# A two-layer fp32 transformer trunk: four slots of split weights, written-out FFN groups, and a new sharing of weight splits between VectorE and GpSimd

## The reference, cut to what matters

```
layer 0:  x = LN(alpha*x + causal_attention(x @ w_qkv) @ w_o)      # 16 heads of 64, partial rotary
layer 1:  x = LN(alpha*x + diff_attention(x @ w_q, x @ w_kv) @ w_o) # 8 heads, two score maps each
both:     up, gate = split(x @ w_in)                                # 1024 -> 2 * 2816
          up = causal_conv3(up) + b;  x = LN(alpha*x + (gelu(up) * gate) @ w_out)
```

## Time and profile before

| what | us |
| --- | --- |
| median of 3 runs | 638.14 (637.22 to 638.71) |
| the profiled execution's own time | 634.84 |
| its span | 633.0 |
| TensorE busy | 613.4 (97% of the span) |
| VectorE busy | 447.4 (71%) |
| ScalarE busy | 335.8 (53%) |
| GpSimd busy | 63.9 (10%) |

### The profile page before, as it was taken

How to read it: one execution, slowest core, us unless ns; L and a number is a source line. 1 busy time by engine, 2 the same in 40 slices (tenths; PEclk the granted TensorE clock), 3 DMA queues, 4 the chain that set the end, 5 groups by cost and what they waited for, 6 DMA issues and landing times. The chain is left out here.

```text
span 633.0 us, 9437 instructions
## 1 busy us (share of the span) xinstructions
PE 613.4 (97%) x3317; PEld 507.1 (80%) x3317; DVE 447.4 (71%) x800; ACT 335.8 (53%) x550; POOL 63.9 (10%) x85
## 2 busy tenths in 40 slices
PE   8999999999999999999889999989999999999995
PEld 6777777798888888889768788768988888888894
DVE  5657477577777777777786676668776777777786
ACT  5667567446444444456326785863545544455450
POOL 4400000420000000000340020044000000000002
PEclk9999999999999999999999999999999999999998
DMA  8973334444555555555368434443634555555521
GB/s 291 338 249 134 134 133 135 134 134 133 200 199 199 199 199 183 174 177 183 146 203 302 160 134 133 134 134 121 211 110 168 188 183 174 176 196 199 199 67 68
DMA packets 68682, 109.67 MB, mean 173 GB/s; under 512 B 2044, under 2 KB 47404, under 8 KB 68140
## 3 DMA queue, kind: packets, MB, share of 16 engines
q1 hardware_dynamic: 68012, 105.09, 49.0%
q0 software_dynamic: 640, 4.20, 1.7%
HBM read 108.23 MB, written 1.05 MB: 173 GB/s over the span
## 5 line engine op out<-in xcount | busy, mean ns | idle before, releaser
L798 DVE TENSOR_TENSOR w_lo<-raw,w_hi 128x2048 fp32r<-128x2048 f32 (+1 forms) x115 | 206.0, 1804 | 68.8 <-ACT w_hi L594 68.8
L594 ACT ACTIVATE w_hi<-raw 128x2048 fp32r<-128x2048 f32 (+1 forms) x125 | 182.0, 1495 | 37.7 <-PE wide L1087 37.7
L1270 PE MATMUL score<-xT,w_hi 128*128 128x512 f32 x288 | 103.2, 401 | 1.5 <-DVE w_lo L798 1.1
L1085 PE MATMUL wide<-w_hi,xT 128*128 128x512 f32 (+1 forms) x256 | 98.4, 384 | 1.9 <-DVE w_lo L856 0.8
L1087 PE MATMUL wide<-w_hi,xT 128*128 128x512 f32 (+1 forms) x256 | 93.4, 365 | 0.0
L1086 PE MATMUL wide<-w_lo,xT 128*128 128x512 f32 (+1 forms) x256 | 93.0, 363 | 0.0
L1272 PE MATMUL score<-xT,w_lo 128*128 128x256 f32 x288 | 80.5, 280 | 0.0
L733 ACT ACTIVATE conv<-up_sum,conv_cols 128x256 f32<-128x256 f32 x36 | 21.7, 602 | 97.1 <-DVE up_sum L997 97.1
L1270 PEld LDWEIGHTS score<-xT,w_hi 128*128 128x128 f32 x288 | 54.0, 188 | 19.2 <-issue 7.2
L1085 PE MATMUL wide<-w_hi,hT_hi 128*128 128x512 f32 x176 | 68.8, 391 | 0.0
L1087 PE MATMUL wide<-w_hi,hT_lo 128*128 128x512 f32 x176 | 68.7, 390 | 0.0
(11 more groups left out here) (181 smaller groups left out, 992.1 us busy)
## 6 DMA issues: line engine op xcount, KB each, us to landing
raw<-in_ffn_w_in SPq DMA_DIRECT2D x44, 1024.0 KB, 5.1
raw<-in_ffn_w_out SPq DMA_DIRECT2D x22, 1024.0 KB, 4.9
raw<-in_a_w_qkv SPq DMA_DIRECT2D x9, 1024.0 KB, 7.0
raw<-in_w_kv_shared SPq DMA_DIRECT2D x8, 1024.0 KB, 5.1
raw<-in_a_w_o SPq DMA_DIRECT2D x4, 1024.0 KB, 4.8
raw<-in_b_w_q SPq DMA_DIRECT2D x4, 1024.0 KB, 5.0
raw<-in_b_w_o SPq DMA_DIRECT2D x4, 1024.0 KB, 4.9
raw<-in_a_w_qkv SPq DMA_DIRECT2D x6, 512.0 KB, 8.7
```

Of the source, the lines that this page charges most:

```text
L594: ins = nc.scalar.activation(w_hi[slot][:, part], raw[slot][:, part], ACT.Copy)
L798: ins = nc.vector.tensor_tensor(w_lo[slot][:, part], raw[slot][:, part], w_hi[slot][:, part].bitcast(F32), ALU.subtract)
L1085: nc.tensor.matmul(dst, a_hi, b_hi, start=start, stop=False, skip_group_check=True)
L1270: nc.tensor.matmul(parts, w_hi[slot][:, cols], xT[:, :, kt, :], start=kt == 0, stop=False, skip_group_check=True)
```

## The change

1. `w_hi` and `w_lo` get four slots (`RING = 4`). `raw` keeps three (`RAW_RING = 3`). The high split of c now waits for TensorE's use of c - 4, the load of c still for the low split of c - 3. In the scheduler of layer 0 the first chunk to be split by the list stays 3 (`FIRST`), which now has a slot without any wait for TensorE.
2. To make room, FFN tiles lie in attention tiles: `hT_hi` and `hT_lo` in `oT_hi` and `oT_lo`, and `conv`, `gelu`, `hidden`, `up_sum`, `gate_sum` in `headT` (named qT and kT in listings).
3. Groups 2 to 9 of the FFN are written out on every engine instead of looped.
4. Splits around the norms: chunk 17 (66) joins the mixer's list of high splits. At n = 1 GpSimd splits both halves of 49 and the second half of 50 before the variance of st = 0, and the first half of 51 before that of st = 1, and none behind `std_inv`. VectorE splits the first half of 50 (`split_shared_lo`), the second half of 51 and all of 52.
5. At the end of layer 0, TensorE's second products of row half 1 run chunk by chunk (chunk 47 first, then 48) instead of column half by column half, its transposes 2 and 3 move ahead of the four products of column group 1 that run early, and VectorE takes one statistics step after a low split of `xT`.

```diff
@@ constants @@
-RING = 3
+RAW_RING = 3
+RING = 4
@@ mixer_schedule @@
-    for c in range(first_chunk + RING, first_chunk + 17):
+    splits = range(first_chunk + (FIRST if A else RING), first_chunk + 18)
+    for c in splits:
         for half in range(2):
-            after[("split_hi", c, half)], after[("split_lo", c, half)] = [], [("split_hi", c, 1)]
+            after[("split_hi", c, half)] = []
+            if c < first_chunk + 16:
+                after[("split_lo", c, half)] = [("split_hi", c, 1)]
...
+        if c - RING in uses:
+            after[("split_hi", c, 0)].append(uses[c - RING])
@@ yoco_trunk @@
-                POOL_SPLITS[2 * layer + 1, st] = ([(c + 2 * st, 0)], [(c + 2 * st, 1)])
+                POOL_SPLITS[2 * layer + 1, st] = ([(c, 0), (c, 1), (c + 1, 1)] if st == 0 else [(c + 2, 0)], [])
...
+        hT_hi = [oT_hi[:, 2 * b:2 * b + 2, :] for b in range(2)]
+        hT_lo = [oT_lo[:, 2 * b:2 * b + 2, :] for b in range(2)]
+        conv = headT[0][:, 0:2, :]
+        gelu = headT[0][:, 2:4, :]
+        hidden = headT[0][:, 4:6, :]
...
@@ SyncE @@
-                elif not isinstance(c, int) or c >= RING:
-                    sp.wait_ge(lo_done, c - RING + 1)
+                elif c >= RAW_RING:
+                    sp.wait_ge(lo_done, c - RAW_RING + 1)
+                slot = c % RAW_RING
@@ ScalarE @@
+                act.wait_ge(raw_in[c % RAW_RING], 16 * (c // RAW_RING + 1))
+                if c >= RING:
                     act.wait_ge(chunk_used, c - RING + 1)
...
                 c = base + QKV_CHUNKS + WO_CHUNKS
-                split_static(c + 1)
                 xT_hi_part(2 * layer + 1, (0, 1))
-                split_static(c + 2)
+                split_hi(c + 2)
                 xT_hi_part(2 * layer + 1, (2, 3))
+                split_hi(c + 3)
...
                 ffn_group(1, "second")
-                with act.Fori(2, GROUPS - 1) as i:
-                    ffn_group(i, "loop")
+                for i in range(2, GROUPS - 1):
+                    ffn_group(i, "middle")
@@ VectorE @@
+            def split_shared_lo():
+
+                part = slice(0, CHUNK // 2)
+                dve.wait_ge(shared_hi_done, 1)
+                nc.vector.tensor_tensor(w_lo[SHARED % RING][:, part], raw[SHARED % RAW_RING][:, part],
+                                        w_hi[SHARED % RING][:, part].bitcast(F32), ALU.subtract).then_inc(shared_lo_done, 1)
...
+                    elif peeled == "last" and cg + RING == SHARED:
+                        split_shared_lo()
@@ TensorE @@
-                        if layer and (cg, kt, st) in ((0, 0, 0), (1, 2, 0)):
+                        if layer and (cg, kt, st) in ((0, 0, 0), (1, 0, 0)):
...
-                for i, st, half in ([(GROUPS - 2, 0, 0), (GROUPS - 2, 0, 1), (GROUPS - 1, 0, 0), (GROUPS - 1, 0, 1)]
-                                    + [(i, 1, half) for half in range(2) for i in (GROUPS - 2, GROUPS - 1)]):
+                tail = [(GROUPS - 2, 1, 0), (GROUPS - 2, 1, 1), (GROUPS - 1, 1, 0), (GROUPS - 1, 1, 1)]
+                if layer + 1 == LAYERS:
+                    tail = [tail[n] for n in (0, 2, 1, 3)]
```

More of the change, by code:

```diff
@@ L128, in mixer_schedule @@
         previous = step
-    for c in range(first_chunk + RING, first_chunk + 17):
-        after[("split_hi", c, 0)].append(uses[c - RING])
+    for c in splits:
+        if c - RING in uses:
+            after[("split_hi", c, 0)].append(uses[c - RING])
     for cg in range(6):
@@ L299, in sem @@
             return ctx.enter_context(nc.semaphore(name))
-        raw = [sb(f"raw{s}", [P, CHUNK]) for s in range(RING)]
+        raw = [sb(f"raw{s}", [P, CHUNK]) for s in range(RAW_RING)]
         w_hi = [sb(f"w_hi{s}", [P, CHUNK], F32R) for s in range(RING)]
@@ L466, in load_in @@
                 def load_in(i, which):
-                    load(ffn_chunk(layer, i, which), ffn_chunk(layer, 1 if not isinstance(i, int) else i, which) % RING,
+                    load(ffn_chunk(layer, i, which),
                          lambda r: r.rearrange("p (k n) -> p k n", k=KT),
@@ L471, in load_out @@
                 def load_out(i):
-                    load(ffn_chunk(layer, i, 2), ffn_chunk(layer, 0 if not isinstance(i, int) else i, 2) % RING,
+                    load(ffn_chunk(layer, i, 2),
                          lambda r: r.rearrange("p (k n) -> p k n", k=2), w_out[:, bass.ds(2 * i, 2), :])
@@ L483, in _ @@
                 load_group(1)
-                with sp.Fori(2, GROUPS) as i:
+                for i in range(2, GROUPS):
                     load_group(i)
@@ L751, in ffn_group @@
                         act.wait_ge(hidden_done, 2 * t + tt + 1)
-                        if tt == 0 and peeled in ("second", "loop"):
+                        if tt == 0 and peeled in ("second", "middle"):
                             act.wait_ge(chunk_used, cg + 2)
@@ L1032, in make_h_lo @@
                                                 ALU.subtract).then_inc(hlo_done, 1)
-                    if peeled == "last":
-                        split_static(cu + RING)
-                    elif not first:
-                        split_after(cu, slot_u)
+                    if not first:
+                        split_lo(cu + RING)
                     if summed:
@@ L1058, in _ @@
                 ffn_group(1, "second")
-                before = steps["n"]
-                LINKS = 2
-                with dve.Fori(2, GROUPS - 1) as i:
-                    steps["i"], steps["per"] = i, LINKS
-                    ffn_group(i, "loop")
-                assert steps["n"] == before + LINKS
-                steps["n"], steps["i"] = before + LINKS * (GROUPS - 3), None
+                for i in range(2, GROUPS - 1):
+                    ffn_group(i, "middle")
                 ffn_group(GROUPS - 1, "last")
@@ L1329, in ffn_group @@
                             for half in range(2):
-                                last = second_product((slot_g + 1) % RING, 0, st, half, start=second)
+                                last = second_product(ffn_chunk(layer, i - 1, 2) % RING, 0, st, half, start=second)
                         last.then_inc(chunk_used, 1)
                 ffn_group(1, "second")
-                with pe.Fori(2, GROUPS - 1) as i:
-                    ffn_group(i, "loop")
+                for i in range(2, GROUPS - 1):
+                    ffn_group(i, "middle")
                 ffn_group(GROUPS - 1, "last")
-                for i, st, half in ([(GROUPS - 2, 0, 0), (GROUPS - 2, 0, 1), (GROUPS - 1, 0, 0), (GROUPS - 1, 0, 1)]
-                                    + [(i, 1, half) for half in range(2) for i in (GROUPS - 2, GROUPS - 1)]):
+                tail = [(GROUPS - 2, 1, 0), (GROUPS - 2, 1, 1), (GROUPS - 1, 1, 0), (GROUPS - 1, 1, 1)]
+                if layer + 1 == LAYERS:
+                    tail = [tail[n] for n in (0, 2, 1, 3)]
+                for i, st, half in [(GROUPS - 2, 0, 0), (GROUPS - 2, 0, 1), (GROUPS - 1, 0, 0), (GROUPS - 1, 0, 1)] + tail:
                     if (st, half) == (0, 0):
```

182 lines of the change are left out of this document (87 added, 95 removed).

## The result

The changed kernel takes 647.02 us (median of 6 runs, 645.61 to 648.13), the kernel before 638.42 beside it (6 runs, 636.27 to 639.41). The ratio is 1.0165, with a 95% interval of 1.0141 to 1.0189: by the medians **8.6 us slower**, where 7.6 was forecast. The two figures do not quite agree: the medians' quotient is 1.0135, just under the interval, and a ratio of 1.0165 would be 10.5 us. Nothing on record tells the two apart. Run once more beside the experiments the ratio was 1.0142 (1.0113 to 1.0170) and the medians 8.8 us apart. So the change costs 8.6 to 10.5 us.

The account below looks back on a forecast made before the run. TensorE, busy for 97% of the span, was taken as the bound, so little could be gained. Terms -4.9 + 3.4 + 8.8 + 0.3 gave +7.6 us, a median of 645.7 us; range 635 to 649.5.

Parts of the forecast that it names:

- FFN groups: FFN groups of both layers: no waits for low splits and no loop cost, -4.9 us, between -2.5 and -6.0.
- Start of mixer 0: Start of layer 0's mixer: k's drain and rotary wait behind chunk 6's load, +3.4 us, bounds +1.4 and +4.0.
- Norms n = 0 and 2: Norms after the mixers: GpSimd's split starts at `std_inv`'s end and holds both of VectorE's L847, +4.4 us each, +8.8 together.
- The end of mixer 1: Last heads of layer 1's mixer: no term of its own; what the prediction did not list was costed at nothing.
- Norm n = 1: Norm between the layers: both L847 collisions go, collisions at `h_lo` and one L847 come, +0.3 us, bounds -3.7 and +1.5.
- I carry differences over to the median: Whole kernel: differences summed against the profiled execution, 634.84 us, were added to the runs' median, 638.14, which is 3.3 above.
- Rival 1: At the norms VectorE keeps the port between its back-to-back instructions: -1.2 us in all, 636.9 us; chance 0.18.
- Rival 2: At n = 0 and 2 GpSimd starts later and L847 goes first, no collision: -5.2 us, 632.9 us; chance 0.14.
- Rival 3: In the FFN groups the fourth slot gives nothing, as loads set the rate: -4.9 falls to -1, 649.6 us; chance 0.07.
- Rival 4: Written-out FFN groups starve TensorE while code is fetched: +14 us on the sum, 659.7 us; chance 0.03.

Follow-up runs that it names:

- e4_written_out: The kernel before with only its FFN group loops written out, three slots and old dealing kept: 634.83 us, ratio 0.9974 to the kernel before.
- e1_norm_wait: The changed kernel, with GpSimd's split of chunk 17 (66) at n = 0 and 2 waiting for both L861 of st = 0: 634.21 us, ratio 0.9976.
- e2_second_half: The changed kernel, with only the second half of GpSimd's split of chunk 17 (66) waiting for both L861 of st = 0: 638.89 us, ratio 1.0051.
- e3_norm_head_wait: The changed kernel with GpSimd's chunk 17 (66) waiting for both L861, and chunk 65 for the last head's scaling: 629.66 us, ratio 0.9893.
- e10_changed_again: The changed kernel once more, word for word, beside the kernel before: 645.17 us, ratio 1.0142.

## Why the prediction was right, and where not

The sign and the mechanism of its largest term are right. The size came out near by luck: two errors cancel. Term by term, on the profiles:

- **FFN groups, -4.9: too large.** It is -2.9 (the four stages of the table with groups 0 to 9), near the low bound of -2.5. The step that failed is "a group then takes 16.53 at best ... so I take 16.65". The shortest pieces of two kinds were put together, as if one group could have both. The changed kernel's 16 groups take 16.79 each, without a wait. Of the 2.9 us, e4_written_out puts 1.6 down to the written-out groups and leaves 1.2 to the rest of the change, the fourth slot above all, nearly all of it in groups 0 and 1. Its measured 1.7 us for writing them out is below the 2.5 us that the prediction estimated from the Trainium skill (Advanced Engine Details and Errata, Control Flow Timing), and of its order. But a fixed price for a branch does not give the split by layer, 0.02 and 1.46 us. The bound of -6.0 was added up wrong too: 16 groups at 16.53 are 5.8 us less, and with the 0.95 at the loops' entry 6.8.
- **Start of mixer 0, +3.4: right in mechanism and, in the first profile, in size** (+3.2). The load was issued at 28.28 and not at 28.9, and chunk 6's high split began at 34.76 and not at 35.9, so k came at 40.69 and not at 41.9. A stretch at the lower clock made up for it. The size varies with the landing, from 1.5 to 5.5 us.
- **Norms n = 0 and 2, +8.8: the mechanism is right, the sum is short.** Every step of it is there: GpSimd's start at `std_inv`'s end, the first L861 held for 2.0, the second held by the second half. e1_norm_wait takes it away and e2_second_half shows the second part alone. The stalls are 4.4 at each norm, as forecast. The two stages cost 13.0. What was missing is the clock: "TensorE stands at these transposes" was priced as the time it stands, and not the slow matmuls behind it, 1.7 us at n = 0 and 2.6 at n = 2. Of these 2.6, 0.9 belong to the stall of the last head (25.66 in e1_norm_wait against 24.72).
- **The end of mixer 1, costed at nothing: the largest miss.** It is 3.4 us of stall plus the clock behind it, 5.3 us in e3_norm_head_wait. "GpSimd's order there does not change, but what it waits for does" was followed for chunk 17 and 66, and not for the chunk before it, 65, whose wait goes in the same manner. At n = 0 nothing is near, at n = 2 the last head is. L965 reads one SBUF tile and was not looked at, since the prediction looked for instructions with two. The Trainium skill (SBUF — State Buffer, SBUF: two separate sides) counts both kinds among those that the shared pair locks, VectorE's in a 2-port mode and those with two SBUF inputs; the 4.66 us for the pair agree.
- **Norm n = 1, +0.3: wrong, it is -3.8**, beyond the low end of -3.7 (in e10_changed_again, with its stall for q, -0.7). Two steps failed. "Behind it stand GpSimd's half of 50 and VectorE's half of 50, so the residual of st = 0 starts near 312.0": GpSimd had to wait for the high split of 50, VectorE's half went first, and the residual started at 317.49, which is 0.45 us later than before against the start of the last group (8.25 us later in the changed kernel) and not 3.2. And "the half of 51, whose high split is ready by 316": that high split waits 5.90 us for TensorE to free a slot, so the collision with L861 does not come. The collision with `h_lo` came, 2.37 for the pair, but it was only half of the forecast one. The first instruction took 2.03 and the second 0.41, since GpSimd's other half of 49 was over and its half of 50 not ready. It cost TensorE 0.2 us and not 1.4.

On the profiles the sum is 12.9 and not 7.6. Against the median it is 8.6, since "I carry differences over to the median" failed as well: the kernel before's own stalls lower its clock in most runs, and the profiled execution was one in which they did not. The profile of before is 3.6 us under its median beside the changed kernel, that of after 0.7 over its own: 4.3 us in all, and they put the number right. That is luck. The sign holds in any case, but 12.9 carried over to the median as the prediction meant it is 651.0, outside its range of 635 to 649.5. For about 1.5 of the 3.6 the runs beside the experiments show the lower clock; for the rest, the six runs of 636.27 to 639.41 have no clock on record.

Rival 1 (VectorE keeps the port between its instructions) falls with the 5.49 us pair and e2_second_half. Rival 2 (no collision at n = 0 and 2) falls with the same rows. Rival 3 (the slot gives the groups nothing) is nearly true for groups 2 to 9, 0.07 us a layer. It is not true for groups 0 and 1, and its price does not hold, since the loop gave the rest. Rival 4 (starved TensorE) falls with e4_written_out.

Not settled: why a group takes 16.79 from start to start each time, in both layers, where one of the kernel before took 16.73. Nothing waits in it. No run tried it.

## What to carry to other kernels

A wait that paces an engine by accident can be what keeps two engines apart. When a buffer is added, list every instruction whose wait it removes, not only the one that was meant, and look what each will then run beside: here three of them, on GpSimd, each met a VectorE instruction that TensorE stood behind. The cure costs one line: let the work with time to spare wait for the work without. With these places and the start of mixer 0 mended the same change gives 1.3% instead of costing 1.4 to 1.65%.

Before carrying a difference of two profiles over to a median, compare the granted clocks of the profiled execution and of the runs.

## What the runs showed of the hardware

- A GpSimd split that waits gets in between two back-to-back VectorE instructions that it collides with, in each pair here: 5.49, 4.66 and 5.53 us against 1.42, 0.48 and 1.42. With one split it is 3.40.
- Beside a GpSimd split, VectorE instructions that read one operand from PSUM ran at full speed (L823, 1.27 for two; L840, 0.69).
- A stall of 2.1 us left TensorE's clock at 1.00 in e2_second_half, and similar ones in e4_written_out were followed by 0.74 and 0.67. Two of 2 us within 3 us of each other, or one of 5, had a granted clock of 0.50 to 0.65 over the next 4 us in every profile here that has them, and the fall came while the second stall, or the long one, still ran, or within 0.2 us of its end. The fall behind the two cost 1.7 us, not much less than one of the stalls.
- The load of chunk 6 into a busy queue landed so differently that the same order of work lost 1.5 to 5.5 us in mixer 0.
